# Both 512-column passes first, then both 256-column passes, in each step of a float32 matmul loop

## Chip, cores and metric

One NeuronCore of one Trainium2 chip runs the whole program. The metric is the device time of that core in microseconds (us). The kernel before was timed three times: 2704.8, 2705.08 and 2706.03 us, median 2705.08.

## What is computed

Two transformer-like blocks work on one sequence of 256 tokens of width 2048, all in float32. Nearly all of the arithmetic is products of the activations with weight matrices; the reference, cut to those:

```python
def first_block(x, ...):                        # 256 x 2048
    h = x + _gla_mixer(_rmsnorm(x), w_in, ..., w_out)   # 2048 x 6160, 2048 x 2048
    h = h + (relu(_rmsnorm(h) @ mlp_w_up) ** 2) @ mlp_w_down   # 2048 x 8192, 8192 x 2048
    return _rmsnorm(h)

def second_block(x, ...):
    proj = rms_norm(x) @ w_in                   # 2048 x 14336
    # attention, a linear recurrence and a short convolution on parts of proj,
    # each through its own output matrix, gated and summed
    x = x + (g_a * y_a + g_b * y_b + g_c * y_c) @ w_out
    x = x + square(relu(rms_norm(x) @ w_mlp_up)) @ w_mlp_down   # 2048 x 8192, 8192 x 2048
    return rms_norm(x)
```

## The kernel before, in words

Every float32 factor is split in two float32r numbers, a high part (the value rounded) and a low part (the rest), and a product is built of three of the four partial products: weight high with activation high, weight high with activation low, weight low with activation high.

Weights come in **units** of 512 x 256 numbers. SyncE loads a unit into one of four slots of `raw`; ScalarE writes its high part (line 787) and VectorE its low part (line 1079) into `wsp`; `w_part(0, slot)` and `w_part(1, slot)` are views of the two. In `wsp` the high parts start at number 16 of a partition's row and the low parts 4148 numbers further on (`HIGHS, LOWS = 16, SLOTS * UK * NB + 52`), so a high tile starts at a multiple of 16 numbers and a low tile 4 numbers past one. The activations stand as `[P, KT, 2, T]` in `xs`, `hs`, `mixs` or `ycs`: for each of 16 groups of 128 features first 256 columns of high parts, then 256 of low parts.

`gemm` is the TensorE program of one **block** of 256 output features: it walks over the units of the block (four in most; 944 units in all), and in a unit over `t` in four **steps** of 128 features. A step holds two halves `j` of 128 output features, each with its own PSUM bank `acc[:, g, j]` (512 columns). For each half there are two **passes**:

- line 507: the high weights of the half stay in the array, 512 columns `x[:, k0 + k]` (high and low activations) stream past into the whole bank;
- line 509: the low weights of the half stay, the 256 columns of high activations stream past and are added to columns 256 to 511 of the same bank.

Each pass is one weight load of 128 x 128 (PEld in the profile) and one matmul. The order before is 512, 256 for `j = 0`, then 512, 256 for `j = 1`; TensorE runs its instructions in the order written. ScalarE later copies the second half of a bank out (`corr`, line 796) and VectorE adds it to the first (line 1089). After the last step of a unit the last matmul raises `unit_used`, which frees the slot's high and low parts for the splits that follow. A unit's first matmul waits for `lo_done` and for the activations.

A block that has `tokens_out=True` (the value projections `gv` and `v`, 12 blocks) swaps the roles, activations stay and weights stream (lines 502 and 504). The first blocks of a stage and the last eight blocks begin with a `spacer`, a 200-column matmul whose result is overwritten (line 482). Between the blocks of the two projection stages stand small float32 matmuls of other work (`hooks`, `hooks2`); one of them, lines 581 and 582, has the same pair of passes as `gemm`, 512 columns and then 256, with weights `wgs[:, k, 0]` and `wgs[:, k, 1]` that both start at a multiple of 128 numbers. The MLP stages (`m1`, `m2`), the branch outputs (`mix`) and the output projections (`go`, `lo`) are loops of blocks with nothing between them but one normalization each (line 523).

Of the kernel before, what the change touches and what calls it, by code (L numbers as in the profile page):

```python
# [20 lines left out]
P = 128  # L21
# [96 lines left out]
def build(nc, a, out, scratch):  # L118
# [15 lines left out]
    def w_part(k, slot):  # L134

        n = UK * NB
        start = HIGHS + k * LOWS + slot * n
        return wsp[:, start:start + n].rearrange("p (t n) -> p t n", t=UK)

    def both_parts(slot, t):  # L140

        row = (slot * UK + t) * NB
        return wsp[:, HIGHS:HIGHS + 2 * LOWS].rearrange("p (k n) -> p k n", k=2)[:, :, row:row + NB]
# [74 lines left out]
    def psum(name, shape):  # L218
        return ctx.enter_context(nc.psum_tensor(name, shape, F32))

    acc = psum("acc", [P, 2, 2, 2, T])
# [254 lines left out]
    def _(pe):  # L476
# [3 lines left out]
        def spacer(to):  # L480

            pe.matmul(to[:, 0:SPACE], xs[:, 0, 0, 0:P], xs[:, 0, 0, 0:SPACE], start=True, stop=True, skip_group_check=True)  # L482

        def gemm(b, units, g, x, ready, k0=0, tokens_out=False, mid=None, before=None, mid_unit=2, spaced=False):

            if not (isinstance(b, int) and b < 2):
                pe.wait_ge(main_read, b - 1)
            for u, (rnd, slot) in enumerate(units):
                if before:
                    before(u)  # L490
                pe.wait_ge(lo_done, SLOTS * rnd + slot + 1)
                for s, v in ready(u):
                    pe.wait_ge(s, v)
                if spaced and u == 0:
                    spacer(acc[:, g, 0, 0])
                for t in range(UK):
                    k = UK * u + t
                    start, stop = k == 0, (u == len(units) - 1 and t == UK - 1)
                    for j in range(2):
                        cols = slice(j * P, j * P + P)  # L500
                        if tokens_out:
                            pe.matmul(acc[:, g, j], x[:, k0 + k, 0, cols], both_parts(slot, t), start=start,  # L502
                                      stop=False, skip_group_check=True)
                            ins = pe.matmul(acc[:, g, j, 1], x[:, k0 + k, 1, cols], w_part(0, slot)[:, t],  # L504
                                            start=False, stop=stop, skip_group_check=True)
                        else:
                            pe.matmul(acc[:, g, j], w_part(0, slot)[:, t, cols], x[:, k0 + k], start=start,  # L507
                                      stop=False, skip_group_check=True)
                            ins = pe.matmul(acc[:, g, j, 1], w_part(1, slot)[:, t, cols], x[:, k0 + k, 0],  # L509
                                            start=False, stop=stop, skip_group_check=True)  # L510
                ins.then_inc(unit_used, 1)
                if mid and u == mid_unit:
                    mid()
# [129 lines left out]
        def straight(name, i, b, rnd, g):  # L643
            mid = first_norm if (name, i) == ("gk", 1) else None
            before = inputs if (name, i) == ("gk", 0) else None
            gemm(b, units_of(rnd, 0, 4), g, xs, split_upto(PAIR0["x1"]), tokens_out=(name == "gv"), mid=mid,
                 before=before, mid_unit=3, spaced=(name, i) != ("gk", 0))
            hooks(name, i)
# [3 lines left out]
        def out_proj(name, x, base):  # L652
            r0, b0 = ROUND0[name], BLOCK0[name]
            with pe.Fori(0, 4) as p:
                for g in range(2):
                    gemm(b0 + 2 * p + g, units_of(r0 + 2 * p + g, 0, 4), g, x, split_upto(base))
# [3 lines left out]
        def mlp(name, x_base, h_base, norm_no, final):  # L660
            def up(c, i, b, rnd, g, first=False):
                gemm(b, units_of(rnd, 0, 4), g, xs, split_upto(x_base),
                     mid=norm(norm_no) if first and g == 0 else None)

            def down(c, i, b, rnd, g, last=False):
                gemm(b, units_of(rnd, 0, 4), g, hs, split_upto(h_base + 8 * c), spaced=last and final)
                if last and final:
                    y_transpose(i)

            mlp_walk(loop, name, up, down)  # L670
# [87 lines left out]
        for j in range(TT):  # L758
            for k in range(2):
                ins = pe.matmul(M[0][:, 0, 2 * j:2 * j + 2], ssq[:, 0, k, j * P:(j + 1) * P], ones[:, 0:2], start=(k == 0),  # L760
                                stop=(k == 1), skip_group_check=True)
# [743 lines left out]
```

## Time and profile before

| what | value |
|---|---|
| median of three runs | 2705.08 us |
| the profiled execution, its own time | 2704.42 us |
| its span, first to last instruction | 2702.6 us |
| TensorE matmuls busy | 2680.7 us, 99% of the span |
| VectorE / ScalarE / GpSimd busy | 66% / 50% / 3% |
| TensorE's granted clock | 0.998 of full speed |
| matmuls of the 512-column pass, line 507 | 7168 |
| matmuls of the 256-column pass, line 509 | 7168 |

A matmul's recorded duration overlaps with its successor's, so durations of TensorE's rows do not add up to time. What can be added is the distance from the start of one matmul to the start of the next. The timeline gives starts to 0.01 us; where a finer figure is wanted it is a stretch's length divided by the number of matmuls of one line in it.

### The profile page before, as it was taken

How to read it: one execution, taken by the hardware profiler on the slowest of the kernel's cores; microseconds unless marked ns; L12 is line 12 of the kernel's file. 1: busy time of each engine (PE TensorE's matmuls, PEld its weight loads, DVE VectorE, ACT ScalarE, POOL GpSimd, SP SyncE). 2: the span in 40 equal slices, each digit the busy share in tenths (PEclk: the TensorE clock that was granted, in tenths of full speed). 3: DMA queues.
4: the chain of work that ended last, by engine and by line, in shares of the span. 5: the costliest groups of instructions: out<-in, count | busy, mean ns of one | idle time of the engine just before them, and what ended most of it. 6: DMA issues, size and time to landing. Idle time of an engine off the chain costs nothing.

```text
span 2702.6 us, 43613 instructions
## 1 busy us (share of the span) xinstructions
PE 2680.7 (99%) x15676; PEld 2362.8 (87%) x15676; DVE 1785.5 (66%) x2056; ACT 1347.1 (50%) x1629; POOL 73.6 (3%) x60
## 2 busy tenths in 40 slices
PE   8999999999999999999999999999999999999998
PEld 7888888888888888888888888888888888888887
DVE  5666776656566567766787666666776565665664
ACT  5546555444444445544675555555554444444443
POOL 1000010000000002200000000000100000000001
PEclk9999999999999999999999999999999999999999
DMA  6794666666566665665556665565666565665653
GB/s 208 165 210 132 193 196 187 190 190 187 187 188 193 189 190 186 194 213 172 164 164 198 192 194 187 191 199 192 194 188 194 187 189 191 187 191 188 187 187 132
DMA packets 507186, 504.45 MB, mean 187 GB/s; under 512 B 17843, under 2 KB 505544, under 8 KB 507096
## 3 DMA queue, kind: packets, MB, share of 16 engines
q1 hardware_dynamic: 505820, 501.60, 59.3%
q10 hardware_dynamic: 1276, 1.63, 1.4%
q8 instruction: 59, 0.97, 0.2%
q14 instruction: 31, 0.25, 0.0%
HBM read 499.50 MB, written 3.67 MB: 186 GB/s over the span
## 4 chain that ended last, share of the span: by engine, by line
PE 97%; DVE 2%; ACT 0%; issue 0%; DMA 0%; POOL 0%; SPq 0%; DVEq 0%; POOLq 0%; ACTq 0%
PE acc L507 59%; PE acc L509 30%; PE acc L502 3%; PE acc L504 2%; DVE wsp L1079 0%; DVE lat L1376 0%; DMA xtok<-in_x 0%; PE misc L612 0%; PE misc L627 0%; PE misc L732 0%; PE acc L482 0%; DVE z L1089 0%; ACT wsp L787 0%; PE misc L594 0%; PE misc L581 0%
## 5 line engine op out<-in xcount | busy, mean ns | idle before, releaser
L1079 DVE TENSOR_TENSOR wsp<-raw,wsp 128x1024 fp32r<-128x1024 f32 x944 | 1167.1, 1244 | 601.0 <-ACT wsp L787 570.9
L507 PE MATMUL acc<-xs,wsp 128*128 128x512 f32 x4224 | 1459.2, 391 | 1.5 <-DVE wsp L1079 1.5
L787 ACT ACTIVATE wsp<-raw 128x1024 fp32r<-128x1024 f32 x944 | 992.8, 1056 | 714.7 <-PE acc L509 626.8
L509 PE MATMUL acc<-xs,wsp 128*128 128x256 f32 x4224 | 1176.3, 278 | 0.0
L507 PEld LDWEIGHTS acc<-xs,wsp 128*128 128x128 f32 x4224 | 793.2, 188 | 171.7 <-DVE wsp L1079 2.4
L507 PE MATMUL acc<-hs,wsp 128*128 128x512 f32 x2560 | 885.4, 391 | 0.0
L509 PEld LDWEIGHTS acc<-xs,wsp 128*128 128x128 f32 x4224 | 793.6, 188 | 0.0
L509 PE MATMUL acc<-hs,wsp 128*128 128x256 f32 x2560 | 714.5, 279 | 0.0
L507 PEld LDWEIGHTS acc<-hs,wsp 128*128 128x128 f32 x2560 | 480.4, 188 | 104.1
L509 PEld LDWEIGHTS acc<-hs,wsp 128*128 128x128 f32 x2560 | 480.7, 188 | 0.0
L796 ACT ACTIVATE corr<-acc 128x512 f32<-128x512 f32 x247 | 147.9, 599 | 390.3 <-PE acc L509 380.4
L1089 DVE TENSOR_TENSOR z<-acc,corr 128x512 f32<-128x512 f32 x247 | 170.7, 691 | 237.8 <-ACT corr L796 237.7
L502 PE MATMUL acc<-wsp,xs 128*128 128x512 f32 x384 | 134.5, 393 | 0.0
L457 POOL TENSOR_TENSOR ssq<-ssq,sq 128x512 f32<-128x512 f32 x40 | 62.6, 1574 | 2574.6 <-ACT sq L807 1893.8
L504 PE MATMUL acc<-wsp,xs 128*128 128x256 f32 x384 | 107.1, 279 | 0.0
L507 PE MATMUL acc<-mixs,wsp 128*128 128x512 f32 x256 | 87.1, 389 | 0.0
L502 PEld LDWEIGHTS acc<-wsp,xs 128*128 128x128 f32 x384 | 72.1, 188 | 16.2
L801 ACT ACTIVATE hs<-z 128x512 f32 (+1 forms) x64 | 40.5, 633 | 90.1 <-DVE z L1294 90.0
L504 PEld LDWEIGHTS acc<-wsp,xs 128*128 128x128 f32 x384 | 72.1, 188 | 0.0
L509 PE MATMUL acc<-mixs,wsp 128*128 128x256 f32 x256 | 70.7, 276 | 0.0
L1273 DVE TENSOR_TENSOR xres<-xres,z 128x512 f32 (+1 forms) x80 | 55.4, 692 | 12.1 <-DVE z L1089 11.8
L507 PEld LDWEIGHTS acc<-mixs,wsp 128*128 128x128 f32 x256 | 48.1, 188 | 10.1
(223 smaller groups left out, 1026.7 us busy)
## 6 DMA issues: line engine op xcount, KB each, us to landing
raw<-in_w_in SPq DMA_DIRECT2D x224, 512.0 KB, 4.3
raw<-in_mlp_w_up SPq DMA_DIRECT2D x128, 512.0 KB, 3.9
raw<-in_mlp_w_down SPq DMA_DIRECT2D x128, 512.0 KB, 4.0
raw<-in_w_mlp_up SPq DMA_DIRECT2D x128, 512.0 KB, 4.0
raw<-in_w_mlp_down SPq DMA_DIRECT2D x128, 512.0 KB, 4.1
raw<-in_gla_w_in SPq DMA_DIRECT2D x96, 512.0 KB, 4.6
raw<-in_gla_w_out SPq DMA_DIRECT2D x32, 512.0 KB, 4.4
raw<-in_w_out SPq DMA_DIRECT2D x32, 512.0 KB, 4.3
```

Source lines behind the costliest of these rows:

```text
L457: ins = pool.tensor_tensor(ssq[:, k], ssq[:, k], sq[:, k], ALU.add)
L502: pe.matmul(acc[:, g, j], x[:, k0 + k, 0, cols], both_parts(slot, t), start=start, stop=False, skip_group_check=True)
L504: ins = pe.matmul(acc[:, g, j, 1], x[:, k0 + k, 1, cols], w_part(0, slot)[:, t], start=False, stop=stop, skip_group_check=True)
L507: pe.matmul(acc[:, g, j], w_part(0, slot)[:, t, cols], x[:, k0 + k], start=start, stop=False, skip_group_check=True)
L509: ins = pe.matmul(acc[:, g, j, 1], w_part(1, slot)[:, t, cols], x[:, k0 + k, 0], start=False, stop=stop, skip_group_check=True)
L787: act.activation(w_part(0, slot), raw[:, slot], ACT.Copy).then_inc(hi_done, 1)
L796: act.activation(corr[:, g], acc[:, g, :, 1], ACT.Copy).then_inc(corr_ready, 1)
L801: act.activation(pair(dst, i)[:, :, 0], src[:], ACT.Copy).then_inc(hi_ready, 1)
L1079: dve.tensor_tensor(w_part(1, slot), raw[:, slot], w_part(0, slot).bitcast(F32), ALU.subtract).then_inc(lo_done, 1)
L1089: dve.tensor_tensor(z[:], acc[:, g, :, 0], corr[:, g], ALU.add).then_inc(main_read, 1)
L1273: own.done(dve.tensor_tensor(pair(xres, i), pair(xres, i), z[:], ALU.add))
```

## The change

In every step of `gemm` whose block is not `tokens_out`, the two 512-column passes come first and then the two 256-column passes, instead of 512, 256, 512, 256. The same 2 x 7168 matmuls with their weight loads are issued, on the same operands (the `tokens_out` blocks have another 2 x 384, which are not touched); no wait, DMA or instruction of another engine changes. The last matmul of a step is in both orders the 256-column pass of `j = 1`.

```diff
                         else:
                             pe.matmul(acc[:, g, j], w_part(0, slot)[:, t, cols], x[:, k0 + k], start=start,
                                       stop=False, skip_group_check=True)
-                            ins = pe.matmul(acc[:, g, j, 1], w_part(1, slot)[:, t, cols], x[:, k0 + k, 0],
+                    if not tokens_out:
+                        for j in range(2):
+                            ins = pe.matmul(acc[:, g, j, 1], w_part(1, slot)[:, t, j * P:j * P + P], x[:, k0 + k, 0],
                                             start=False, stop=stop, skip_group_check=True)
                 ins.then_inc(unit_used, 1)
```

On TensorE, at the head of the first block that begins with a spacer (`gk`, second block; the same pattern stands in all the other blocks), before:

```order
L482 MATMUL acc<-xs 128x200 [waits split_done,lo_done]
L507 MATMUL acc<-xs,wsp 128x512
L509 MATMUL acc<-xs,wsp 128x256
L507 MATMUL acc<-xs,wsp 128x512
L509 MATMUL acc<-xs,wsp 128x256
L507 MATMUL acc<-xs,wsp 128x512
L509 MATMUL acc<-xs,wsp 128x256
```

and after, where "x2" stands for two in a row, `j = 0` and `j = 1` (the pass of line 509 is on line 511 there):

```order
L482 MATMUL acc<-xs 128x200 [waits split_done,lo_done]
L507 MATMUL acc<-xs,wsp 128x512 x2
L511 MATMUL acc<-xs,wsp 128x256 x2
L507 MATMUL acc<-xs,wsp 128x512 x2
L511 MATMUL acc<-xs,wsp 128x256 x2
L507 MATMUL acc<-xs,wsp 128x512 x2
```

The first 256-column pass of a step has moved behind the second 512-column pass. The waits stay in front of the same matmul, the first of the unit.

## Rows read from the trace of the kernel before

**Rows 1.** The page: busy shares, the granted clock in 40 slices, the chain of waits.
```profile
PE 2680.7 (99%) x15676; PEld 2362.8 (87%) x15676; DVE 1785.5 (66%) x2056; ACT 1347.1 (50%) x1629; POOL 73.6 (3%) x60
...
PEclk9999999999999999999999999999999999999999
...
PE 97%; DVE 2%; ACT 0%; issue 0%; DMA 0%; POOL 0%; SPq 0%; DVEq 0%; POOLq 0%; ACTq 0%
```

**Rows 2.** TensorE's waits: who waited for whom, total us, times, longest.
```profile
PE acc L507 <- DVE wsp L1079: 1.5, 2, 1.3
```

**Rows 3.** Line 507 by stretch: us, PE and PEld busy (count), clock, DMA share.
```profile
494.00:1115.00 621.00, 621.00 (x1793) 336.16 (x1792) 1.00 0.61 190
...
1485.00:1973.00 488.00, 488.00 (x1436) 269.41 (x1436) 1.00 0.60 192
...
1984.00:2596.00 612.00, 612.00 (x1766) 331.17 (x1766) 1.00 0.61 190
```

**Rows 4.** Timeline of TensorE (start us, us): one normalization between two steps.
```profile
412.32 0.39 PE L507 MATMUL acc<-xs,wsp 128*128 128x512 f32 x1
412.55 0.28 PE L509 MATMUL acc<-xs,wsp 128*128 128x256 f32 x1
412.67 1.02 PE L523 MATMUL misc<-ssq,ones 128*128 128x256 f32 x4
```

**Rows 5.** Timeline, a projection block: its second and its last pair.
```profile
1330.87 0.39 PE L507 MATMUL acc<-xs,wsp 128*128 128x512 f32 x1
...
1341.42 0.38 PE L702 MATMUL misc<-k,q 128*128 128x128 f32 x2
```

**Rows 6.** The same of the block that follows it.
```profile
1344.38 0.39 PE L507 MATMUL acc<-xs,wsp 128*128 128x512 f32 x1
...
1355.13 0.27 PE L702 MATMUL misc<-k,q 128*128 128x128 f32 x1
```

**Rows 7.** Timeline in the first MLP, matmuls.
```profile
599.80 0.39 PE L507 MATMUL acc<-xs,wsp 128*128 128x512 f32 x1
600.03 0.28 PE L509 MATMUL acc<-xs,wsp 128*128 128x256 f32 x1
600.15 0.39 PE L507 MATMUL acc<-xs,wsp 128*128 128x512 f32 x1
```

**Rows 8.** The same stretch, weight loads.
```profile
600.04 0.19 PEld L507 LDWEIGHTS acc<-xs,wsp 128*128 128x128 f32 x1
600.15 0.19 PEld L509 LDWEIGHTS acc<-xs,wsp 128*128 128x128 f32 x1
600.38 0.19 PEld L507 LDWEIGHTS acc<-xs,wsp 128*128 128x128 f32 x1
```

**Rows 9.** Timeline in the `mix` stage, matmuls.
```profile
1599.76 0.39 PE L507 MATMUL acc<-xs,wsp 128*128 128x512 f32 x1
1599.99 0.28 PE L509 MATMUL acc<-xs,wsp 128*128 128x256 f32 x1
1600.10 0.39 PE L507 MATMUL acc<-xs,wsp 128*128 128x512 f32 x1
```

**Rows 10.** Timeline of the pair loop on lines 581 and 582.
```profile
37.44 0.40 PE L581 MATMUL misc<-xs,wgs 128*128 128x512 f32 x1
37.67 0.28 PE L582 MATMUL misc<-xs,wgs 128*128 128x256 f32 x1
37.79 0.40 PE L581 MATMUL misc<-xs,wgs 128*128 128x512 f32 x1
38.03 0.28 PE L582 MATMUL misc<-xs,wgs 128*128 128x256 f32 x1
...
41.33 0.40 PE L581 MATMUL misc<-xs,wgs 128*128 128x512 f32 x1
```

**Rows 11.** Timeline of a `tokens_out` block, five pairs apart.
```profile
105.23 0.40 PE L502 MATMUL acc<-wsp,xs 128*128 128x512 f32 x1
...
106.99 0.40 PE L502 MATMUL acc<-wsp,xs 128*128 128x512 f32 x1
```

**Rows 12.** Timeline, equal matmuls in a row: four of 256 and four of 128 columns.
```profile
1315.83 1.03 PE L732 MATMUL misc<-lat,wax 128*128 128x256 f32 x4
...
2618.16 0.60 PE L681 MATMUL misc<-ident,h 128*128 128x128 f32 x4
```

**Rows 13.** Groups of TensorE by shape, those two lines: busy us, mean ns of one.
```profile
L732 PE MATMUL misc<-lat,wax 128*128 128x256 f32 x32 | 8.2, 379 | 0.0
L681 PE MATMUL misc<-ident,h 128*128 128x128 f32 x32 | 4.8, 272 | 3.6 <-ACT ytok L1053 3.6
```

## The prediction

> **What bounds the kernel now.** I read the chain of waits first: 97% of it is TensorE, and matmuls are on record in 99% of the span [rows 1]. Then TensorE's own waits: for its weights it waited 1.5 us in the whole run [rows 2], and the granted clock is 1.00 in each long stretch, the 2.4 GHz level [rows 1, 3]. So the time is the rate at which TensorE starts matmuls. The change touches only that: it alters the order of 2 x 7168 of its matmuls and no wait, and VectorE (66% busy) and ScalarE (50%) have room on both sides of it. A unit's slot is freed after the same matmul as before, so loads and splits are released no earlier or later within a step.
>
> The rate must be read from start to start. A **pair** (one 512-column pass and one 256-column pass) has two speeds. In the first MLP 1793 pairs take 621 us, 0.3463 us each, in the second 1766 take 612 us, 0.3465 each; in the output loops 1436 take 488 us, 0.3398 each [rows 3]. It is not data or the clock: two projection blocks that follow each other on the same tiles take 10.55 and 10.75 us for 31 pairs, 0.3403 and 0.3468 [rows 5, 6]. The pair keeps its speed through a loop of hundreds of pairs, and can change it at a small interruption such as the normalization at 412.67 us: before it pairs go at 0.340, and the whole rest of the MLP goes at 0.3465 [rows 3, 4]. I call them the short pace and the long pace. By the starts of the stretches about 2740 of the 7168 pairs go at the short pace (24 before that normalization, 256 in `go`, 1152 in `mix`, 256 and 24 after it, 64 at the very end, two thirds of the 1408 in the projection blocks) and 4430 at the long one. The mean pair is (2740 x 0.340 + 4430 x 0.3465) / 7168 = 0.3440 us, all pairs 2466 us, and the 237 us that are left of the span are not touched.
>
> At the long pace the 512-column matmul takes 0.23 us up to the next start and the 256-column one 0.12 [rows 7]; at the short pace 0.23 and 0.11 [rows 9]. The load of the next matmul's weights starts with each matmul, within 0.01 us [rows 7, 8]: each stream covers exactly one load, the next one's, and none is fetched two ahead.
>
> **The change, part by part.** No instruction is added or removed, so nothing is priced by a count of instructions. What changes is which load lies behind which stream. Before: behind each 512-column stream the load of low weights, behind each 256-column stream the load of high weights. After, in one step: behind the 512 of `j = 0` the high weights of `j = 1`; behind the 512 of `j = 1` the low weights of `j = 0`; behind the 256 of `j = 0` the low weights of `j = 1`; behind the 256 of `j = 1` the high weights of the next step. So out of the four, one 512-column stream now has a high load behind it, and one 256-column stream a low one. The other two keep what they had.
>
> Does it matter? If each stream only paid for its own columns, the sum of a step would be the same. The trace has one loop of the same shape in which both loads start at a multiple of 16 numbers, as the high tiles do and the low tiles don't: lines 581 and 582. Eleven of its pairs take 41.33 - 37.44 = 3.89 us, 0.3536 each [rows 10]. A `tokens_out` block, whose stationary tiles also lie on such multiples, takes 1.76 us for five, 0.352 each [rows 11]. That is 7 ns more than a pair at the long pace, 14 more than one at the short, 9.6 more than the mean pair, and in the rows it stands mostly with the 512-column stream (0.23 and 0.24, where 256 has 0.12 as at the long pace) [rows 10]. I put the whole difference on a 512-column stream that has an aligned load behind it: **+9.6 ns** per step, since a step now has one of them. Against it stands the 256-column stream that now covers a low load. If the shifted tile is what makes the low load cheap, it is cheap there too. What it can gain is bounded by nothing on one side, and by 0.117 less 0.109 on the other, 8 ns: four equal 128-column float32 matmuls take 0.60 us with a last one of 0.272, so 0.109 from start to start, and their 256-column neighbours need 0.217, so these are the nearest rows to a stream of about this length with a 128 x 128 load behind it [rows 12, 13]. I take half, **-4 ns**, near the difference between the two paces for this stream [rows 7, 9].
>
> Sum: +5.6 ns per step, 3584 steps: +20 us on the profiled execution's 2704.42 us, and its median lies 0.7 us above: 2725 us.
>
> The bounds of a step, from the nearest rows however far. Below: two equal matmuls in a row could go as float32 ones of equal size do. Four of 256 columns take 1.03 us with a last one of 0.379, 0.217 from start to start, with 0.109 for the short ones [rows 12, 13]: 0.652 per step against 0.688 now, -129 us. Those are of another number format and I see no reason why float32r streams should lose all of their surplus, as no pair in the trace is under 0.3398; so the end that I use is that pair, 2 x 0.340 per step. Above: both pairs of a step as in lines 581 and 582, 0.707 per step, (0.3536 - 0.3440) x 7168 = +69 us.
>
> The Trainium skill, page "TensorE: Matmul & The Clock Gate", section "Step-by-step: what each phase is for", says that moving columns and weights come in over independent read ports, so that a load takes nothing from the running stream. In its section "Back-to-back issue gap" a warm matmul costs its columns at 2.4 GHz and 2.5 ns, which would be an estimated 0.325 us for the pair in any order. The rows speak against it as a full account (0.340 to 0.354 for one shape, by pace and by tile), but what it gives for this change is a time that doesn't depend on the order, and that is the second rival.
>
> **The rivals.**
>
> *It gets faster: the new order settles at the short pace.* The two paces show that up to 6.5 ns per pair are not owed to work but to how loads and streams fall together. A new order has its own paces. If all pairs went at 0.340, the gain is 4430 x 6.5 ns = 29 us: 2676; if one stream of four stays dear, half of that, 2690. For it: 4430 of 7168 pairs go at the dearer pace, so there is more to win than to lose by a fresh draw; low loads move under the short streams, where there is least spare time behind a load. Against it: lines 581 and 582 show that a high load behind a 512-column stream goes at a pace dearer than both. Decides from: a step under 0.686.
>
> *It stays the same: the order is free.* If the surplus belongs to each matmul by its columns, a step is the same sum: 2705, and only blocks that change their pace move it, by 10.4 us at most for a third of the projection blocks and the ends. For it: 512 and 256 carry surplus in both states. Against it: the surplus differs with the tile [rows 6, 10].
>
> *Much slower: both pairs go as lines 581 and 582 do.* 0.350 to 0.3536 per pair, 2748 to 2774. For it: two loads of like kind (high, high; low, low) now follow each other as in that loop. Against it: half of the streams keep the load that they had.
>
> *The change doesn't do what it says.* The order of TensorE's instructions shows it done in all blocks but the 12 `tokens_out` ones; there is nothing between the passes that could put them back.
>
> **How the numbers follow.** Slower as forecast, 2711 to 2745: 0.41. Much slower, beyond that: 0.09. Faster: 0.32, spread over 2676 to 2699. The same within 0.2% (5.4 us, about what a measurement of this kernel can tell from no change), 2699.7 to 2710.5: 0.18. The predicted time is that of the likeliest case, 2725; taken alone it has 2711 to 2745. The range of 8 in 10 goes from 2676, all pairs at the short pace, to 2750 and leaves out the much slower end and what would be under the shortest pair of the trace. Faster 0.32, same 0.18, slower 0.50: cases of both signs are open, since no row shows two equal float32r matmuls after one another.
>
> **What the profile after would show.** The counts of lines 507 and of the moved pass over the MLP stretches give the step: 0.694 us on average if I am right, against 0.693 in the MLPs and 0.680 in the `mix` stage before; the loss should show above all in the `mix` and output loops, which go at the short pace now. In the timeline the 512 of `j = 0` should take 0.24 to the next start and that of `j = 1` 0.23; the 256 of `j = 0` 0.11, that of `j = 1` 0.12. If both 512 take the same and both 256 too, which load is covered doesn't matter, and my step on alignment is wrong. If the step in the MLPs is under 0.686, the short pace has won. If TensorE has new waits for VectorE, or the clock is under 1.00, the time is not what this sum is about. My forecast is wrong above all if the surplus of lines 581 and 582 comes from something else than where their weights start.

## The result

The changed kernel takes 2752.56 us (median of four runs, 2752.01 to 2753.75), the kernel before 2704.94 us in the same comparison. The ratio is 1.0175 with a 95% interval of 1.0163 to 1.0187: 1.75% slower, 47.6 us. The forecast was slower, 2725 us with a range of 2676 to 2750; the direction held, the size was more than twice the 20 us of the sum, and the time lies 2.6 us past the range.

TensorE does the same work in more time and waits for nobody new. The page of the kernel after, its busy shares and the chain of waits:

```profile
span 2750.3 us, 43613 instructions
...
PE 2729.0 (99%) x15676; PEld 2376.8 (86%) x15676; DVE 1785.8 (65%) x2056; ACT 1347.6 (49%) x1629; POOL 73.6 (3%) x60
...
PEclk9999999999999999999999999999999999999999
...
PE 99%; DVE 0%; ACT 0%; DMA 0%; issue 0%; POOL 0%; DVEq 0%; POOLq 0%; ACTq 0%
```

VectorE and ScalarE are busy for the same time as before [rows 1], the clock is the same, and the one wait of TensorE for split weights is 1.0 us, against 1.5 [rows 2]:

```profile
PE acc L507 <- DVE wsp L1081: 1.0, 1, 1.0
```

The rate is read as before, from the matmuls of line 507 in three stretches: the first MLP, the `mix` stage, the second MLP (stretch in us, its length, PE busy with the count, PEld busy with the count, clock, DMA share, GB/s). The kernel before:

```profile
430.00:1100.00 670.00, 670.00 (x1933) 362.57 (x1934) 1.00 0.61 190
1520.00:1950.00 430.00, 430.00 (x1266) 237.43 (x1265) 1.00 0.60 193
2060.00:2550.00 490.00, 490.00 (x1414) 265.19 (x1414) 1.00 0.61 189
```

and after:

```profile
430.00:1100.00 670.00, 600.78 (x1909) 293.25 (x1910) 1.00 0.61 188
1520.00:1950.00 430.00, 385.52 (x1226) 188.29 (x1226) 1.00 0.58 186
2060.00:2550.00 490.00, 439.36 (x1397) 214.42 (x1396) 1.00 0.60 187
```

A pair took 0.3466, 0.3397 and 0.3465 us before; after, half a step takes 0.3510, 0.3507 and 0.3508. There is one pace for the whole program now, above both old ones: 4.4 ns per pair more in the MLPs and 11 ns more where the short pace was. (The trace has 3152 windows of eight steps with no other matmul between them; 3091 of them go at 0.351 a pair and 52 at 0.352 or 0.353.) With the shares of the prediction, 4430 x 4.4 ns + 2740 x 11 ns = 50 us, and the span grew by 47.7. That accounts for the whole loss to within 2 us.

The paces are steady. By the trace's start times the kernel before takes 11.093 or 11.094 us for each of 44 stretches of 32 pairs, one behind the other, in the first MLP and 10.880 us for each of 37 in the `mix` stage; the changed one takes 11.228 to 11.241 us for such a stretch in both. DMA and the other engines work beside all of them, and none of it shows, so nothing in these stretches points at them as the cause of a pace.

Inside a step, matmuls and then weight loads of the kernel after in the first MLP (start us, us; "x2" are two in a row):

```profile
599.91 0.63 PE L507 MATMUL acc<-xs,wsp 128*128 128x512 f32 x2
600.38 0.40 PE L511 MATMUL acc<-xs,wsp 128*128 128x256 f32 x2
600.61 0.63 PE L507 MATMUL acc<-xs,wsp 128*128 128x512 f32 x2
601.08 0.40 PE L511 MATMUL acc<-xs,wsp 128*128 128x256 f32 x2
...
602.72 0.39 PE L507 MATMUL acc<-xs,wsp 128*128 128x512 f32 x1
```

```profile
600.15 0.42 PEld L511 LDWEIGHTS acc<-xs,wsp 128*128 128x128 f32 x2
600.50 0.31 PEld L507 LDWEIGHTS acc<-xs,wsp 128*128 128x128 f32 x2
600.84 0.42 PEld L511 LDWEIGHTS acc<-xs,wsp 128*128 128x128 f32 x2
```

As before, a load starts with the stream that covers it [rows 7, 8], so 600.15 is also the start of the second 512-column stream and 600.50 that of the second 256-column one. The four distances are 0.24, 0.23, 0.12 and 0.11 us, and four steps (599.91 to 602.72) take 2.81, 0.7025 each. In the next step the first 512-column stream takes 0.23 (600.61 to 600.84) and the second 0.24 (to 601.08). The two together take 0.47 in both steps, where two of before took 0.46 [rows 7, 9]. The rounding to 0.01 us is as large as the difference between them; the mean over the some 950 steps of 430 to 1100 us, from the trace's start times, tells them apart. It is 0.2333 us for the 512 of `j = 0` and 0.2344 for that of `j = 1`, against 0.2292 before in the same stretch, and 0.1158 and 0.1186 for the two 256s, against 0.1175. Both 512-column streams have become dearer, by 4 and 5 ns; the surplus does not sit on one stream.

### The profile page after: what moved, and what is told of

The parts are those of the page before. It is cut to its first block, busy times and chain, and to the rows that moved or that the text cites. A ratio compares the mean times of both kernels' runs of the same rounds, so it can differ in the third digit from the quotient of the medians.

```text
span 2750.3 us, 43613 instructions
## 1 busy us (share of the span) xinstructions
PE 2729.0 (99%) x15676; PEld 2376.8 (86%) x15676; DVE 1785.8 (65%) x2056; ACT 1347.6 (49%) x1629; POOL 73.6 (3%) x60
## 4 chain that ended last, share of the span: by engine, by line
PE 99%; DVE 0%; ACT 0%; DMA 0%; issue 0%; POOL 0%; DVEq 0%; POOLq 0%; ACTq 0%
PE acc L507 61%; PE acc L511 31%; PE acc L502 3%; PE acc L504 2%; PE misc L614 0%; PE misc L629 0%; PE misc L734 0%; PE acc L482 0%; DMA xtok<-in_x 0%; PE misc L553 0%; PE misc L596 0%; PE misc L583 0%; PE misc L525 0%; PE misc L631 0%; PE misc L705 0%; PE misc L720 0%
## 5 line engine op out<-in xcount | busy, mean ns | idle before, releaser
L507 PE MATMUL acc<-xs,wsp 128*128 128x512 f32 x4224 | 1331.7, 396 | 1.0 <-DVE wsp L1081 1.0
L511 PEld LDWEIGHTS acc<-xs,wsp 128*128 128x128 f32 x4224 | 792.4, 188 | 192.3
L511 PE MATMUL acc<-xs,wsp 128*128 128x256 f32 x4224 | 839.9, 281 | 0.0
L507 PE MATMUL acc<-hs,wsp 128*128 128x512 f32 x2560 | 806.0, 396 | 0.0
L507 PEld LDWEIGHTS acc<-xs,wsp 128*128 128x128 f32 x4224 | 649.2, 189 | 1.8 <-DVE wsp L1081 1.2
L511 PEld LDWEIGHTS acc<-hs,wsp 128*128 128x128 f32 x2560 | 480.1, 188 | 116.3
L511 PE MATMUL acc<-hs,wsp 128*128 128x256 f32 x2560 | 508.8, 280 | 0.0
L507 PEld LDWEIGHTS acc<-hs,wsp 128*128 128x128 f32 x2560 | 393.3, 189 | 0.0
L507 PE MATMUL acc<-mixs,wsp 128*128 128x512 f32 x256 | 80.6, 396 | 0.0
L511 PE MATMUL acc<-mixs,wsp 128*128 128x256 f32 x256 | 50.9, 280 | 0.0
```

The lines of the kernel that those rows point to most:

```text
L511: ins = pe.matmul(acc[:, g, j, 1], w_part(1, slot)[:, t, j * P:j * P + P], x[:, k0 + k, 0], start=False, stop=stop, skip_group_check=True)
```

## The experiments

Every run's pace is given as the length of a stretch divided by the count of the 512-column pass in it, for the same three stretches; the rows shown have the columns named above. A stretch also counts matmuls that it cuts, so a pace read in this way can be up to 0.0005 us low. One profile and one time were taken of each unless an interval is given, against a kernel before of 2705.3 to 2705.8 us beside them. In `wsp` and in all activation tiles a partition's row starts at a multiple of 64 numbers, so a tile's **start** can be told as its remainder by 64: activations 0, high tiles 16, low tiles 4 (16 + 4148 = 4164) in both kernels.

### Where the low tiles start, in both orders (e1, e2)

```diff
-    HIGHS, LOWS = 16, SLOTS * UK * NB + 52
+    HIGHS, LOWS = 16, SLOTS * UK * NB + 48
```

e1 is the order of before with this edit:

> The order of before (512, 256, 512, 256), but the low parts start 4144 numbers behind the high ones instead of 4148, so that low tiles start at a multiple of 16 numbers like the high ones. Theory A (where the load that lies behind a stream starts is what costs): each pair becomes like the pairs of lines 581 and 582, 0.3536 us instead of 0.344 on average, 2705 + 69 = 2774 us. Theory B (equal lengths after one another are what costs, whatever is loaded): nothing changes, 2705 us but for blocks that change between 0.340 and 0.3465, 2677 to 2723.

e2 is the changed order with it:

> The changed order (512, 512, 256, 256) with the same edit, low tiles at a multiple of 16 numbers. Theory A: all four loads of a step are now alike in both orders, so it costs what the order of before costs with this edit, 2774 us, 0.707 us a step. Theory B: as the changed kernel, 2753 us, 0.702 us a step.

Measured: e1 2706.2 us, e2 2792.5 us. Line 507 in e1:

```profile
430.00:1100.00 670.00, 670.00 (x1972) 369.88 (x1971) 1.00 0.63 195
1520.00:1950.00 430.00, 430.00 (x1266) 237.43 (x1265) 1.00 0.61 194
2060.00:2550.00 490.00, 490.00 (x1401) 263.00 (x1401) 1.00 0.60 187
```

and in e2:

```profile
430.00:1100.00 670.00, 595.90 (x1880) 289.36 (x1880) 1.00 0.59 183
```

e1 has 0.3398, 0.3397 and 0.3498 us a pair: the short pace is untouched and is now also that of the first MLP, and the long one has become 0.350. Theory A, on which the prediction's sum was built, said 0.3536 for all pairs. It is refuted, and so is theory B as it was put: e2 has 0.3564 a pair, 40 us above the changed kernel, so the start of the low tiles does matter in the new order. (That e1's total is that of the kernel before is an accident of which stretch has which pace.)

### PSUM banks (e3)

The lengths take turns, but from the second step of a block on the 256-column pass belongs to the other half:

```diff
-  512 of j=0, 256 of j=0, 512 of j=1, 256 of j=1
+  512 of j=0, 256 of j=1, 512 of j=1, 256 of j=0
```

> Lengths take turns as before, but after the first step of a block the 256-column pass that follows a 512-column one is that of the other half: 512 of j=0, 256 of j=1, 512 of j=1, 256 of j=0. Every matmul writes another PSUM bank than the one ahead of it, as in the changed kernel, and behind each 512 lies a low load as before. Theory A and B: as before, 2677 to 2723 us, 0.340 to 0.3467 a pair. Rival C (the change of PSUM bank between two matmuls costs): as the changed kernel, 2753 us, 0.351 a pair.

Measured: 2704.8 us. Its 512-column pass, on line 511 there:

```profile
430.00:1100.00 670.00, 670.00 (x1934) 362.61 (x1933) 1.00 0.61 190
1520.00:1950.00 430.00, 430.00 (x1266) 237.46 (x1265) 1.00 0.60 193
```

0.3464 and 0.3397, both paces in the same places as before. But the expectation above misreads its own order. The halves go 0, 1, 1, 0, and the bank still changes at every second matmul, as before (0, 0, 1, 1); only the places of the changes have moved, from behind a 256-column pass to behind a 512-column one. That this costs and gains nothing is shown. In the changed kernel the halves go 0, 1, 0, 1 and every matmul writes another bank than its predecessor; e3 does not test that. Rival C falls only with e6 and with e13 to e16 below.

### Is the pace only a state? (e4)

The kernel before with one more spacer in each MLP:

```diff
-                     mid=norm(norm_no) if first and g == 0 else None)
+                     mid=norm(norm_no) if first and g == 0 else None, spaced=first and g == 1)
```

> The kernel before with one more 200-column spacer at the head of the second block of each MLP. If the pace of a pair (0.340 or 0.3465) is only how the stream of loads and matmuls has fallen together, kept until something interrupts it, the 200 columns should bring it from the long pace to the short one, as the spacers between projection blocks do, and the MLPs stay there: about 3900 pairs times 6.6 ns = 26 us less, 2679 us. If the pace of the MLPs belongs to their data, tiles or loads, nothing changes: 2705 us.

Measured: 2679.98 us (2679.13 to 2680.26, four runs), ratio to the kernel before 0.9906 with an interval of 0.989 to 0.9923. Line 507:

```profile
430.00:1100.00 670.00, 670.00 (x1971) 369.85 (x1972) 1.00 0.63 195
1520.00:1950.00 430.00, 430.00 (x1266) 237.37 (x1266) 1.00 0.61 194
2060.00:2550.00 490.00, 490.00 (x1443) 270.56 (x1442) 1.00 0.62 193
```

0.3399, 0.3397 and 0.3396: both MLPs go at the short pace to their ends after two extra matmuls of 200 columns. Around the one in the first MLP:

```profile
413.79 0.39 PE L507 MATMUL acc<-xs,wsp 128*128 128x512 f32 x1
...
415.53 0.39 PE L507 MATMUL acc<-xs,wsp 128*128 128x512 f32 x1
...
415.87 0.26 PE L482 MATMUL acc<-xs 128*128 128x200 f32 x1
...
417.02 0.39 PE L507 MATMUL acc<-xs,wsp 128*128 128x512 f32 x1
...
418.72 0.39 PE L507 MATMUL acc<-xs,wsp 128*128 128x512 f32 x1
```

Five pairs ahead of it take 1.74 us (0.348 each) and five behind it 1.70 (0.340). The forecast of 26 us is met (25 us), and the kernel beats both others. So which of its two paces the order of before takes does not belong to data, tiles or loads; it is a state that a small interruption sets. The changed order has the same spacers at the heads of its projection blocks and of the last eight blocks, and yet it has 0.351 in all three stretches; no second pace was seen in it.

### Which half of the regrouping costs? (e5, e6)

The change groups two things at once: stream lengths, and kinds of load. Two kernels do one of them alone, with the first step of each block left in the old order. Written as length and load in turn:

```diff
 before        512 high, 256 low,  512 high, 256 low
 changed       512 high, 512 high, 256 low,  256 low
+e5            512 high, 256 high, 512 low,  256 low
+e6            512 high, 512 low,  256 high, 256 low
```

(The load named is the one that a stream needs, and it lies behind the stream ahead.) Weights and columns are paired differently from the reference in these two, so their products are not its products; the counts and sizes of loads and matmuls are the same. The halves `j`, and with them the PSUM banks, go 0, 1, 0, 1 in e5 and 0, 0, 1, 1 in e6.

> After the first step of each block the lengths take turns (512, 256, 512, 256), but the loads come as in the changed kernel (high, high, low, low); the weights and columns are mismatched on purpose, so the products are not the reference's, while counts and sizes are the same. Theory B (equal lengths after one another cost): the pair stays at 0.340 to 0.3467 us, 2677 to 2723 us. Theory A2 (two loads of one kind after one another cost): as the changed kernel, 0.351 us a pair, 2753 us.

> The opposite: after the first step of each block the lengths are 512, 512, 256, 256 but the loads take turns (high, low, high, low); again mismatched on purpose, same counts and sizes. Theory B: as the changed kernel, 0.351 us a pair, 2753 us. Theory A2: 0.340 to 0.3467, 2677 to 2723 us.

Measured: e5 2743.6 us, e6 2754.8 us. The 512-column pass (line 512 in both) in the first MLP, e5 and then e6:

```profile
430.00:1100.00 670.00, 670.00 (x1917) 358.92 (x1916) 1.00 0.59 188
```

```profile
430.00:1100.00 670.00, 602.42 (x1907) 296.73 (x1908) 1.00 0.59 187
```

0.3495 and 0.3513 us. Either half alone costs most of what both cost together (0.3510, against 0.344 for the mean pair of before). e6 does so with the bank changes of the kernel before, so these are not what costs there. Both theories fall as they stood: the cost is not a sum of one price for equal lengths and one for equal loads.

### The price of equal streams (e7, e8)

All passes with 512 columns, and all with 256:

```diff
-  passes of 512 (high) and 256 (low) columns
+  e7: 512 and 512;  e8: 256 and 256
```

> All passes but those of tokens_out blocks have 512 columns (the low pass too, so results are not the reference's), loads high, low in turn. It gives the price of a 512-column stream after its like. If a stream pays only for its own columns and load, 0.227 to 0.229 us as in the kernel before, about 14336 x 0.228 + 237 = 3506 us. If equal lengths in a row are what is dear, 0.233 to 0.236 as in the changed kernel, 3590 us and more.

> The same with 256 columns in all of those passes (the main product with the low activations is left out). The distance inside a unit is what counts, the whole may be held back by VectorE or the loads. If a stream pays only for its own columns and load, 0.113 to 0.117 us. If a 256-column stream is too short for the load behind it and the next in a row has to wait for it, 0.117 to 0.125.

Measured: e7 3477.1 us, e8 2095.3 us. The first step of each block keeps its 256-column passes in e7, which the 3506 us left out. In e8 TensorE waits for splits and the clock is 0.99, so only the distance inside a run of matmuls is used. A row of nine in e7 and one of eighteen in e8, from the timelines (start us, us from the first start to the last end):

```profile
599.77 2.23 PE L512 MATMUL acc<-xs,wsp 128*128 128x512 f32 x9
```

```profile
599.73 2.28 PE L515 MATMUL acc<-hs,wsp 128*128 128x256 f32 x18
```

With 0.39 and 0.28 us for the last one, (2.23 - 0.39) / 8 = 0.230 and (2.28 - 0.28) / 17 = 0.118 us from start to start. If prices were per stream, a step would be 2 x 0.230 + 2 x 0.118 = 0.696 us in any order. The old order goes under that (0.680) and the new one over it (0.702). With high and low loads in turns, equal lengths in a row are hardly dear in themselves: 0.230 is 1 ns over the 512-column distance of the long pace (0.229), under the 0.233 at which the expectation would have called them dear, and 0.118 is the 256-column distance of the long pace.

### Kind of load, or start? (e9, e10)

e5's and e6's orders with the edit of e1 (LOWS + 48, low tiles at remainder 0, high ones still at 16):

> The order of e5 (lengths in turns, loads high, high, low, low, mismatched on purpose) with low tiles at a multiple of 16 numbers. Theory F (a load counts only by where its tile starts within 16 numbers, and a pace is a pattern of lengths and starts that repeats): high and low loads are now alike, so this is the order of before with aligned lows: 0.340 or 0.350 us a pair and nothing else, 2677 to 2749 us. Theory G (grouping the kinds costs as such): as without the edit or dearer, 0.350 and more everywhere, with another pattern than e1 has.

> The order of e6 (lengths 512, 512, 256, 256, loads in turns, mismatched on purpose) with low tiles at a multiple of 16 numbers. Theory F: the same as e2, 0.713 us a step, with distances near 0.238, 0.233, 0.124, 0.118 in turn, 2792 us. Theory G: as e6, 0.703 a step, or another value than e2's.

Measured: e9 2768.3 us, e10 2760.5 us. First MLP, line 512, e9 and e10:

```profile
430.00:1100.00 670.00, 670.00 (x1898) 356.58 (x1897) 1.00 0.60 185
```

```profile
430.00:1100.00 670.00, 603.43 (x1902) 297.07 (x1900) 1.00 0.61 187
```

0.3530 and 0.3523 us, where theory F wanted 0.340 or 0.350 of e9, and e2's 0.3564 of e10. So remainders by 16 are not what counts. It was also the wrong test of "alike": by 64, high and low tiles still start differently there (16 and 0).

### Other starts for the two orders (e11, e12)

LOWS + 56, low tiles at remainder 8, in e4 (e11) and in the changed kernel (e12):

> e4 (the order of before and a spacer in each MLP) with low tiles 8 numbers past a multiple of 16 instead of 4. Theory F: the short pace needs only lengths in turns with one start for each length, so 0.340 a pair stays possible; the long pace may be another (0.3467 with 4 numbers, 0.350 with none). If the spacers still bring the short pace: 2680 us; if not, up to 2750.

> The changed kernel with low tiles 8 numbers past a multiple of 16 instead of 4. Theory F: the pattern of a step has two lengths and two starts in the same places, so no pace under 0.346 a pair; between 0.702 (4 numbers) and 0.713 (none) a step, 2750 to 2795 us. If the start of low tiles is the cause, there should be one at which the grouped order is as cheap as the other: 0.680 to 0.693, 2677 to 2723.

Measured: e11 2733.3 us, e12 2744.8 us. Line 507 in e11, first and second MLP:

```profile
430.00:1100.00 670.00, 670.00 (x1933) 362.84 (x1933) 1.00 0.62 190
...
2060.00:2550.00 490.00, 490.00 (x1397) 262.17 (x1396) 1.00 0.61 187
```

and in e12:

```profile
430.00:1100.00 670.00, 600.14 (x1916) 293.66 (x1915) 1.00 0.61 188
```

With this start the old order has 0.3466 and 0.3508, and no 0.340 in any stretch, although the spacers are there; the new order has 0.3497. The claim that the short pace needs only lengths in turns is refuted: it also needs certain starts. For e12 a step between 0.702 and 0.713 was expected and 0.6994 was measured by the count (0.700 by the start times of whole blocks), 5 us under the least total. That this start would not bring the new order under 0.346 a pair held; one at which it is as cheap as the old one (0.680 to 0.693 a step) was not found.

### All starts equal (e13 to e16)

High and low tiles both at remainder 0, the four orders in turn:

```diff
-    HIGHS, LOWS = 16, SLOTS * UK * NB + 52
+    HIGHS, LOWS = 0, SLOTS * UK * NB + 64
```

> The order of before with the high tiles at a multiple of 64 numbers and the low ones too (HIGHS 0, LOWS 4160; before, 16 and 4 numbers past one). Theory F2 (a load counts by its start within 64 numbers, 256 bytes): this is lines 581 and 582 everywhere, so 0.3533 us a pair is one of its paces, beside it perhaps 0.340 or 0.350: 2774 us if all pairs take it. If starts don't matter at all: 0.340 and 0.3467, 2677 to 2723.

> The changed order with both kinds at a multiple of 64 numbers. If lengths in pairs cost by themselves, with loads that are all alike: no pair under 0.350, 2745 us and more, in one pace for the whole program. If it is the loads' starts in pairs that cost: as e13, since the starts are all the same now.

> The order of e5 and e9 (lengths in turns, loads high, high, low, low, mismatched on purpose) with both kinds at a multiple of 64 numbers. Theory F2: loads can't be told apart, so only paces that e13 has, to 0.01 us a step. Theory G (the kind or the jump from tile to tile costs as such): dearer than e13, near 0.700 to 0.707 a step.

> The order of e6 and e10 (lengths 512, 512, 256, 256, loads in turns, mismatched on purpose) with both kinds at a multiple of 64 numbers. Theory F2: the same distances in the same sequence as e14. Theory G: another sequence, 0.703 to 0.713 a step.

Measured: e13 2739.1, e15 2738.6; e14 2735.4, e16 2738.7 us. The 512-column pass in e13:

```profile
430.00:1100.00 670.00, 670.00 (x1934) 362.44 (x1933) 1.00 0.62 190
1520.00:1950.00 430.00, 430.00 (x1218) 228.68 (x1218) 1.00 0.59 186
2060.00:2550.00 490.00, 490.00 (x1415) 265.10 (x1414) 1.00 0.62 189
```

and in e15, other kinds of load under the same lengths:

```profile
430.00:1100.00 670.00, 670.00 (x1934) 362.40 (x1933) 1.00 0.62 190
1520.00:1950.00 430.00, 430.00 (x1218) 228.68 (x1218) 1.00 0.58 186
2060.00:2550.00 490.00, 490.00 (x1415) 265.10 (x1414) 1.00 0.61 190
```

The counts are the same to the matmul. e14 and then e16, lengths in pairs:

```profile
430.00:1100.00 670.00, 604.04 (x1924) 292.87 (x1924) 1.00 0.62 189
```

```profile
430.00:1100.00 670.00, 608.21 (x1922) 296.92 (x1921) 1.00 0.61 189
```

0.3482 and 0.3486 us. What is left between them lies at the first step of each block, which in e16 has the old order and in e14 the new: by the start times a block of 16 steps in the first MLP takes 11.147 us in e14 and 11.160 in e16, and from the third step on the distances are the same to 1 ns in the same sequence, 0.697 us a step. Some 220 blocks of 13 ns make 3 of the 3.3 us between the totals. So with equal starts the kind of load is indifferent, as theory F2 said: a load counts by where its tile starts within 64 numbers (or 32, which was not told apart), and by nothing else that was tried. The `mix` stage of e13 has 0.3530, the pace of lines 581 and 582 [rows 10], whose tiles have these very starts; e13's MLPs have 0.3464. And with equal starts the lengths in pairs are not dear: 0.348 lies between the two paces of the lengths in turns. Neither branch of e14's expectation came out, not 0.350 and more, and not a pace of e13 either.

The same four runs settle the PSUM banks. The halves go 0, 0, 1, 1 in e13 and e16 and 0, 1, 0, 1 in e14 and e15. e15 changes the bank at every matmul and e13 at every second one, with the same counts; e14 and e16 differ in the same way and have the same distances. So with equal starts a bank change at every matmul costs nothing. With the starts of before only e6 bears on it, which loses without one; for e5's share of the loss it was not told apart from the loads.

All paces that were seen in the stretches, us per pair, the first number of a start being that of high tiles:

| order | 16, 4 | 16, 0 | 16, 8 | 0, 0 |
|---|---|---|---|---|
| in turns (before) | 0.340, 0.3465 | 0.340, 0.350 | 0.3466, 0.351 | 0.3464, 0.353 |
| lengths and loads in pairs (changed) | 0.351 | 0.356 | 0.350 | 0.348 |
| loads in pairs | 0.3495 | 0.353 | not tried | 0.3464, 0.353 |
| lengths in pairs | 0.351 | 0.352 | not tried | 0.3486 |

## Why the prediction was right or wrong

**What bounds the kernel: right.** No wait, clock or other engine moved; the whole difference is in the distances between TensorE's matmuls.

**That a pair has two paces and keeps one until it is disturbed: right**, and e4 shows it by an intervention that was forecast to 1 us. The shares of 2740 and 4430 hold too: with the measured paces they give the loss to within 2 us (block by block the trace has 2616 pairs at the short pace, which changes that sum by under 1 us), and the loss is largest, as expected, in the stretches that had the short pace.

**The failed step: "I put the whole difference on a 512-column stream that has an aligned load behind it", +9.6 ns, with -4 ns for the 256-column stream.** The sum was +5.6 ns per step; measured are 0.702 - 0.688 = +14 ns. It failed in two ways. First, lines 581 and 582 were read as a price of one load under one stream. e1 made the low tiles start at a multiple of 16, as the prediction's words wanted it, and left the 0.340 where it was; e13 shows that these two lines are one pace of one sequence of lengths and starts, which has a cheaper pace (0.3464) beside it. Second, there is no price per stream to be added: e7 and e8 give 0.696 for a step as a sum, and real steps of the same content run from 0.680 to 0.713. The surplus stands on both 512-column streams, 0.2333 and 0.2344 against 0.2292 at the long pace. The one with the high load behind it, on which the prediction put everything, is the cheaper of the two. The 256-column stream that covers a low load is cheaper than its neighbour, as forecast (0.1158 against 0.1186), but it gains 1.7 ns on the long pace and not 4, and the other one loses 1.1. The prediction's own sign that its step on alignment is wrong was that both 512 take the same and both 256 too: the 512s do within 1.1 ns, and the 256s are 2.8 ns apart, so the load that is covered does matter, but by far less than the 9.6 ns. The timeline, rounded to 0.01 us, could not show this.

**The rivals.** "Faster" is refuted: the new order has a pace of its own, one, and it is not the short one; "more to win than to lose" counted only the paces of the old order, as if a new one would draw from the same two. "The order is free" is refuted by the result, and with it what the prediction made of a formula of the Trainium skill (page "TensorE: Matmul & The Clock Gate", section "Back-to-back issue gap"). The formula, which the page gives for the gap of an isolated matmul, goes by columns alone and so gives one time for all orders; the measured steps differ by 5% for the same columns. "Much slower" had the right size, 0.350 to 0.3536 a pair and 2748 to 2774 us, and got 0.09. Its reason, two loads of like kind in a row, is half of the truth: e5 shows that this alone does give 0.3495, but e6 gives 0.3513 with the loads still in turns, and with equal starts the pairing of loads costs nothing (e15 against e13) and that of lengths stays within the paces of the old order (0.348).

**The range** ended at 2750 although the dearest rows of the trace reached to 2774. Three different sequences (lines 581 and 582, the `tokens_out` blocks, the pair itself) each had a pace of its own there, between 0.340 and 0.354, so a fourth sequence should have been given that whole spread.

**What stays open.** Shown is that the sequence of stream lengths and of tile starts decides which paces exist, and that an interruption picks one of them. Why the sequence of before with its starts has 0.340 and the regrouped one only 0.351 is not shown: no row tells what loads and streams contend for. The start of the activations, the same for all, was not varied, nor were other widths of spacer. All runs but the changed kernel and e4 are single ones; their paces are read over hundreds of matmuls.

## What to carry to other kernels

When TensorE issues one weight load per short float32r stream and is busy throughout, count its matmuls per stretch before and after every edit: several stable paces for one and the same loop, here up to 3% apart, can hide or fake a gain, and a short dummy matmul in front of a long loop may move it to the better one for nothing (0.94% here). A regrouping that is neutral by its counts is not neutral there, and its price can't be added up from streams measured in another sequence. Where tiles start in SBUF belongs to the same set of choices and must be tried together with the order.

## What was unexpected of the hardware

- One loop with unchanged instructions has more than one stable pace, kept for hundreds of matmuls: 0.340 and 0.3465 us a pair; with low tiles 4 numbers earlier 0.340 and 0.350; with both kinds at multiples of 64 numbers 0.3464 and 0.353.
- A 16-byte shift of the low weight tiles is worth 40 us in the regrouped order (e2 against the changed kernel) and nothing to the short pace of the old one (e1).
- A steady pace repeats to the nanosecond: 44 stretches of 32 pairs in a row, each 11.093 or 11.094 us (first MLP of the kernel before).
- Exchanging high and low loads, with a change of PSUM bank at every matmul in place of every second, changes not one matmul in the PE counts of three stretches once their tiles start alike (e13, e15).
- Streams of 512 float32r columns in a row with a load each take 0.230 us, streams of 256 0.118 (e7, e8), while taking turns they can go at 0.340 for both together, less than the sum of 0.348.
